# A two-block transformer forward pass on one Trainium2 core: context products ahead of x's, four fixed experts with a ring of 16, and two groups of loads issued inside the attention loop

## What is computed

```python
# first block, for each of 2 layers:
#   x += 0.5 * ffn(rmsnorm(x));  x += attention mix of three branches;  x += 0.5 * ffn(rmsnorm(x))
# x = rmsnorm(x) * final_g
# second block:
hx = _modulate(_rmsnorm(x, norm1_g), sh1, sc1)        # from c @ w_ada
hc = _modulate(_rmsnorm(ctx, norm1_g), csh1, csc1)    # 256 context tokens, from c_ctx @ w_ada
qa, ka, va, qr, kr, vr, gr = split(hx @ w_in)         # x: all seven parts
ka_c, va_c, kr_c, vr_c = parts of split(hc @ w_in)    # context: the parts that x attends to
x_new = x + gt1 * (concat([attention(qa, [ka_c, ka], [va_c, va]), retention(...)]) @ w_out)
y = _hier_moe(_modulate(_rmsnorm(x_new, norm2_g), sh2, sc2), ...)  # top-1 group, top-2 of its 8 experts
out = _rmsnorm(x_new + gt2 * y, final_norm_g)
```

## Time and profile before

| | |
|---|---|
| median of 3 runs | 2082.81 us (2081.47 to 2091.58) |
| the profiled execution's own time | 2081.88 us |
| its span | 2080.1 us |
| PE busy | 1984.5 us (95%) |
| DVE busy | 1132.3 us (54%) |
| ACT busy | 655.0 us (31%) |
| loaded and stored by DMA | 475.56 MB, mean 229 GB/s |

### The profile page before, as it was taken

The page is one execution under the profiler, slowest core; times in us unless marked ns, Lnnn a source line. Parts: engine busy times, 40 slices in busy tenths (PEclk is TensorE's granted clock), DMA queues, the critical chain, the costliest instruction groups (busy, mean ns, idle before and its releaser), DMA issues.

```text
span 2080.1 us, 33242 instructions
## 1 busy us (share of the span) xinstructions
PE 1984.5 (95%) x13991; PEld 1629.1 (78%) x13991; DVE 1132.3 (54%) x1939; ACT 655.0 (31%) x980; POOL 0.2 (0%) x4
## 2 busy tenths in 40 slices
PE   7999999998999999999999999979997998989997
PEld 7999998887999999999888999968665444434443
DVE  6665669845655665666984556554475222222222
ACT  4433436614333533343661433320332000000001
POOL 0000000000000000000000000000000000000000
PEclk9999999999999999999999999999899999999999
DMA  7798553448776677655244877612305999999995
GB/s 223 246 356 244 170 172 95 132 132 233 223 220 194 205 220 215 196 170 173 92 132 135 260 222 214 166 41 81 142 23 203 421 422 420 422 420 422 421 421 246
DMA packets 273950, 475.56 MB, mean 229 GB/s; under 512 B 28182, under 2 KB 234064, under 8 KB 249224
## 3 DMA queue, kind: packets, MB, share of 16 engines
q1 hardware_dynamic: 267148, 471.75, 65.8%
q10 hardware_dynamic: 6652, 1.65, 0.6%
HBM read 472.22 MB, written 7.95 MB: 231 GB/s over the span
## 4 chain that ended last, share of the span: by engine, by line
PE 78%; DMA 16%; DVE 3%; ACT 1%; ACTq 1%; issue 0%; SPq 0%; DVEq 0%
PE ps L692 77%; DMA ring_zone<-in_moe_w_up_dram 16%; PE ps L992 1%; ACTq L395 1%; PE ps L1128 0%; DVE hl L1706 0%; DVE xT L1713 0%; DVE WL L1695 0%; DMA PT<-in_norm_g_dram 0%; SPq L618 0%; ACT WH L1370 0%; DVE xT L1758 0%; ACT gT L1501 0%; DVE xT L1889 0%; DVE h2l L2266 0%
## 5 line engine op out<-in xcount | busy, mean ns | idle before, releaser
L1695 DVE TENSOR_TENSOR WL<-W,WH 128x1024 fp32r<-128x1024 f32 x372 | 452.3, 1223 | 324.7 <-ACT WH L1370 324.3
L692 PE MATMUL ps<-hh,WH 128*128 128x256 f32 x2128 | 604.7, 284 | 18.8 <-DVE WL L1695 13.1
L692 PE MATMUL ps<-hl,WH 128*128 128x256 f32 x2128 | 595.8, 280 | 0.0
L692 PE MATMUL ps<-hh,WL 128*128 128x256 f32 x2128 | 595.4, 280 | 0.0
L1370 ACT ACTIVATE WH<-W 128x1024 fp32r<-128x1024 f32 x372 | 391.0, 1056 | 469.1 <-PE ps L692 429.0
L692 PEld LDWEIGHTS ps<-hh,WH 128*128 128x128 f32 x2128 | 401.8, 189 | 32.5 <-issue 21.1
L692 PEld LDWEIGHTS ps<-hl,WH 128*128 128x128 f32 x2128 | 401.9, 189 | 0.2
L692 PEld LDWEIGHTS ps<-hh,WL 128*128 128x128 f32 x2128 | 401.6, 189 | 0.0
L692 PE MATMUL ps<-ring_over,XT 128*64 128x512 f32 x896 | 228.2, 594 | 31.0 <-DMA ring_zone<-in_moe_w_up_dram 14.3
L692 PEld LDWEIGHTS ps<-ring_over,XT 128*64 128x64 f32 x896 | 77.1, 137 | 176.1 <-issue 176.0
L692 PE MATMUL ps<-hid_h,WH 128*128 128x256 f32 x704 | 200.5, 285 | 0.0
(11 more groups left out here) (330 smaller groups left out, 2194.9 us busy)
## 6 DMA issues: line engine op xcount, KB each, us to landing
ring_over<-in_moe_w_gate_dram SPq DMA_DIRECT2D x64, 1024.0 KB, 20.4
ring_zone<-in_moe_w_down_dram SPq DMA_DIRECT2D x64, 1024.0 KB, 18.8
ring_over<-in_moe_w_up_dram SPq DMA_DIRECT2D x48, 1024.0 KB, 22.5
W<-in_ffn_w_gate_dram SPq DMA_DIRECT2D x88, 512.0 KB, 4.9
W<-in_ffn_w_up_dram SPq DMA_DIRECT2D x88, 512.0 KB, 4.4
W<-in_ffn_w_down_dram SPq DMA_DIRECT2D x88, 512.0 KB, 3.9
W<-in_w_in_dram SPq DMA_DIRECT2D x78, 512.0 KB, 4.4
W<-in_w_gate_dram SPq DMA_DIRECT2D x48, 512.0 KB, 3.7
```

Source lines behind the costliest of these rows:

```text
L692: ins = nc.tensor.matmul(o, lhsT, rhs, start=start, stop=stop, skip_group_check=True, **kw)
L1695: v.tensor_tensor(low, W[:, i % RAW, :], high.bitcast(F32), ALU.subtract).then_inc(low_ready, 1)
```

## The change

Three edits, made together.

1. **Context first.** The context is loaded into `gT`, normed, transposed and modulated inside `ffn(1, 1)`, blocks 5 to 7, and split into `hc_h` and `hc_l`. `w_in2` becomes a split kind, so that all 13 products are `mm3`. They run in the order of `ORDER`, which begins with the context's 3 and 6. The two norms of x are made one: `block_squares` forms the squares of x and of x times its gain, `block_sums` adds both up, and `modulated` makes the high and low part of the modulated x. The normed x itself (`normed_residual`) is made later, after the product at position 5. `decay(0)` moves ahead of the last two products.
2. **Four fixed experts, 16 places.** Blocks 0 to 3 belong to experts 0 to 3. `RING` is 16: one place more in the zone, and `hl`, `mT`, `hT` as places. SP waits for the table only at piece 24. The position of a token's slot no longer needs the running sum over experts (tokens beyond the 64th of an expert get a number far away); the running sum moves into `block_table`, and `move_tokens` gives slots their true numbers after the first quad.
3. **Loads.** Layer 1's `load_na` is issued by SP within the pieces of `w_branch` of layer 0; the first two `ada_unit`s of `ffn(l, 1)` are issued among the pieces of `w_o`.

```diff
-RING, RING_OVER, RING_RAW = 12, 7, RAW // 2
+RING, RING_OVER, RING_ZONE, RING_RAW = 16, 7, 6, RAW // 2
+ORDER = (3, 6, 2, 5, 8, 7, 0, 1, 4, 11, 12, 10, 9)
+CHUNK = {0: 0, 1: 1, 2: 2, 3: 2, 4: 3, 5: 4, 6: 4, 7: 5, 8: 5, 9: 6, 10: 6, 11: 7, 12: 8}
+SIDE = {1: [("ss", 3)], 3: [("ss", 2)], 4: [("rot", 2)], 5: [("rot", 5)], 7: [("ss", 0)], 8: [("ss", 1), ("rot", 0)],
+        9: [("rot", 1)], 10: [("rot", 4)]}
+CONTEXT_AT = 5
+RESIDUAL_AT, DECAY_AT = 5, 10
-SPLIT = ("ffn_gate", "ffn_up", "ffn_down", "w_in", "w_gate")
+SPLIT = ("ffn_gate", "ffn_up", "ffn_down", "w_in", "w_gate", "w_in2")
 # SP
                     if n == RING_OVER:
                         sp.wait_ge(m_ready, 2 * KD + 4)
+                    if n == RING_OVER + RING_ZONE - 1:
+                        sp.wait_ge(lg_ready, 2)
+                    if n == RING - 1:
+                        sp.wait_ge(x_turned, 1)
...
+                    if kind == "w_o" and half == 0 and c % 2 == 0:
+                        load_ada(first_ada(key, 1) + c // 2)
+                    if plan[i] == ("w_branch", 0, 8, 0):
+                        sp.wait_ge(qk_free, NA_H)
+                        load_na(sp, 1)
...
-            first_experts(range(RING_OVER, RING))
+            first_experts(range(RING_OVER, RING_OVER + RING_ZONE - 1))
             first_experts(range(RING_RAW))
+            first_experts(range(RING_OVER + RING_ZONE - 1, RING))
+            fixed_end = plan.index(("moe_gate", FIXED, 0, 0))
+            stream(moe_at + RING, fixed_end)
             sp.wait_ge(table_ready, 1)
 # PE, in ffn
+                    if (l, i, b) == (1, 1, CONTEXT_AT + 1):
+                        turn_context()
 # PE, second block
+            pe.wait_ge(ctx_low, 4)
+            sums = begin()
+            turns.step()
+            for p, g in enumerate(ORDER):
+                c = CHUNK[g]
+                bank = begin()
+                if p == CHUNK_FIRST[c]:
+                    held[c] = [take("w_in2")]
+                product(held[c], bank, g, 0)
+                if p == 0:
+                    block_sums(sums)
+                if p == CHUNK_FIRST[c]:
+                    held[c].append(take("w_in2"))
+                product(held[c], bank, g, 1)
+                idx[g] = turns.step()
+                if p == CHUNK_LAST[c]:
+                    done_pair(2)
 # ACT
+            def block_squares():
+                nc.scalar.activation(rt[:, 2, 1:2], eps[:, :], ACT.Sqrt)
+                for b in range(4):
+                    act.wait_ge(x_tiles, due(x_tiles))
+                    for k in (2 * b, 2 * b + 1):
+                        nc.scalar.activation(nT[:, k, :], xT[:, k, :], ACT.Square, scale=col("final_g", k))
+                    nc.scalar.activation(mT[:, 2 * b:2 * b + 2, :], xT[:, 2 * b:2 * b + 2, :], ACT.Square)\
+                        .then_inc(sq_ready, 1)
...
+            def round_modulated():
+                for k in range(KD):
+                    act.wait_ge(h_plain, due(h_plain))
+                    nc.scalar.activation(hh[:, k, :], nT[:, k, :], ACT.Identity, bias=MOD[:, k, 0:1])\
+                        .then_inc(norm_h, 1)
...
-                if l + 1 < DEPTH:
-                    load_na(act, l + 1)
 # DVE
+            def modulated():
+                take()
+                dve.wait_ge(rms, due(rms))
+                give(v.reciprocal(rstd[:, :], rstd[:, :]))
+                given()
+                for k in range(KD + 1):
+                    if k < KD:
+                        v.scalar_tensor_tensor(out=nT[:, k, :], in0=xT[:, k, :], scalar=G1[:, 0, k:k + 1],
+                                               in1=rstd[:, :], op0=ALU.mult, op1=ALU.mult).then_inc(h_plain, 1)
+                    if k:
+                        dve.wait_ge(norm_h, due(norm_h))
+                        v.scalar_tensor_tensor(out=hl[:, k - 1, :], in0=nT[:, k - 1, :], scalar=MOD[:, k - 1, 0:1],
+                                               in1=hh[:, k - 1, :].bitcast(F32), op0=ALU.add, op1=ALU.subtract)\
+                            .then_inc(h_ready, 1)
```

## The result

The changed kernel takes 2051.52 us (median of 4 runs, 2049.62 to 2052.42), the one before 2085.24 us beside it (4 runs, 2081.47 to 2091.58): ratio 0.984, 95% interval 0.982 to 0.986, 1.6% faster. The forecast was 2033 us with a range of 2018 to 2047. The direction is right; the time lies 4.5 us above the range. The profiled execution takes 2051.78 us with a span of 2050.0, 30.1 us less than before, where the prediction has 49.5.

The account below looks back on a forecast made before the run. PE was taken as the bound up to the experts, the DMA stream of expert weights from there. Terms -9.5 + 5.5 - 28.3 - 6 - 2.6 - 8.6 = -49.5 from 2081.88 gave 2032.4, predicted 2033 us, range 2018 to 2047.

Parts of the forecast that it names:

- loads of tables: Start of `ffn(0, 1)`: issuing the loads from SP ends PE's wait for the split; -9.5 us, bounds -9.5 and 0.
- context into `ffn(1, 1)`: Context's transposes, router row and a 2.3 us wait added in `ffn(1, 1)`; +5.5 us, bounds +3.3 and +9.
- feed-forward's end to last product: Last feed-forward matmul to end of 13 split products: 125.8 us become 97.5; -28.3 us, bounds -33 and -18.
- attention's start: Last product to first retention product: decay matrices already made, later steps perhaps at higher clock; -6 us, bounds -3 and -9.
- routing: From expert counts to slots, five of DVE's 16 operations remain; -2.6 us, bounds -3 and -1.5.
- expert stream: Expert weights: restart 3.9 us after the first expert matmul, 172 pieces instead of 176; -8.6 us, bounds -13 and -4.
- rival B: Experts: stream not started earlier, through late places or loads; only routing's -2.6 stays of the end; 2041 us, chance 0.08.
- A: Projections bound by DVE, splits behind side work; 2043 us with the -18 bound, chance 0.17.
- C: Layer 1's table loads on SP delay the branch weights, PE waits up to 8 us; 2041 us, chance 0.07.
- D: Faster: no late split (-5.1) and no wait in block 6 (-2.3); 2025 us, chance 0.12.
- the wait in block 6: In `ffn(1, 1)`, bank turns tie PE to DVE while the context is transposed; PE waits 2.3 us.
- E: Slower: more than 32 expert blocks, so eight more run, 48 pieces, 120 us; about 2152 us, chance 0.02.

Follow-up runs that it names:

- the square first: Changed kernel with ACT squaring piece 3 before its eight roundings of the modulated x, instead of after; 2034.53 us, ratio to the kernel before 0.976.
- -32: Square moved first, `eps` and `eps_sq` in one tile, `neglam` and `subg` in one: later tiles 32 bytes lower than in the kernel before; 2058.31 us.
- -96: Square moved first, `eps`/`eps_sq` in one tile, `neglam`, `subg`, `rstd_of`, `rtok` in one: later tiles 96 bytes lower than in the kernel before; 2024.81 us.
- its shifted twin: Changed kernel with one more unused 4-byte tile behind `eps_sq`, later tiles 64 bytes higher than in the kernel before; 2072.50 us.

## Why the prediction was wrong

By its steps, forecast and measured in the profiled executions:

| step | forecast | measured |
|---|---|---|
| loads of tables | -9.5 | -9.45 |
| context into `ffn(1, 1)` | +5.5 | +4.8 |
| feed-forward's end to last product | -28.3 | -17.9 |
| attention's start | -6 | -5.1, and +0.8 up to the routing |
| routing | -2.6 | -1.9 |
| expert stream | -8.6 | -6.9 |
| equal work in the first block | 0 | +4.4 |
| start of the program | 0 | +1.1 |

- **Feed-forward's end to last product** is the step that failed, by 10.4 us, and beyond its own bound of -18. Its order of events came true: product 2 starts 22.1 us behind the last hidden matmul, as forecast, PE waits 3.6 us there (forecast 4.3), and late splits and a late `Z` cost 3.5 (forecast 5.1). What the step did not have is the clock, a term that it put at nothing. It costed every matmul at full rate although it put an idle stretch of its own ahead of ten products. The half clock took 9.0 us in products 2 and 5 (23.15 against 14.17) and 1.5 in one at 1441 (7.26 against 5.73 for 48 matmuls). The earlier trace rows show 0.88 and 0.79 behind PE's idle stretches: the rows were there, and no term was made of them. With the wait gone the stage gives -37.8 to the first retention product, 3.7 of them the wait itself; the other -34.1 are the -33.9 that the prediction has for the same stretch. So the order of events and the waits were right, and the clock was the missing term. That the remainder meets the forecast to 0.2 us is partly luck: the waits came out 2.3 us shorter than forecast (3.6 and 3.5 against 4.3 and 5.1), and the work between them longer by about as much.
- **Attention's start**: the 7.8 us are 2.7 (forecast 2.2). The 1.5 us that a higher clock should have given came out as a loss of 0.8, since the clock fell at 1469 for 6.8 us; with the square first the stretch gives 2.4 (98.3 us against 100.7).
- **Equal work** had no term and cost 4.4 us, set by 32 bytes in the list of tiles. No row of the kernel before prices it.
- **Expert stream**: 1.7 us short. The restart came 4.5 us behind the first expert matmul, not 3.9, and the 172 pieces took 437.8 us, 3.7 more than 428.4 + 5.7 instead of the 3 forecast. A fault that doesn't show in the sum is the price of the restart: the term counts 1.7 us for it (3.9 instead of 5.6) and rival B puts the loss of the early start at 8.6, while the runs show 1.0 us for a restart 5.0 us later, within the scatter. The places are worth 8.7.
- **Tables, context, routing** were right within 0.7 us. In the routing, DVE's chain gave its 2.5 us (from the count to the gather 5.8 us, 8.3 before), but the gather that follows took 5.9 instead of 5.4, a larger part of it at half clock. PE waits nowhere between 440 and 510. SP was held 16 us by the 16 transfers (11 forecast), within its lead.
- **Rivals.** A (DVE the bound) is out: moving two items took most of the waits away. B and C did not occur: the restart came before the table, and no branch weight was late. D neither: late splits and `Z` cost 3.5 us and the wait in block 6 0.9 (2.3 forecast). E neither: there are 64 gate transfers again.

## What to carry to other kernels

When a forecast puts an idle stretch of some us on TensorE, price the matmuls behind it at the lower clock as a second case; the wait may be the smaller part, and reordering one 0.4 us instruction, or filling the stretch with needless matmuls, can win more than the wait. Take out such waits first, and then look for late work on the vector engine. When equal work gets slower everywhere by a per cent after an edit, compare the addresses of the tiles before looking for anything else.

## What was not expected of the hardware

- The pace of the split matmuls changes when tiles move in SBUF by 32 bytes: 192.9 to 198.6 us for the same stage at the same clock, up to 34 us from the first root to the last hidden matmul (1341.4 us at -32 against 1307.3 at -96). No rule for the best place came out of seven places; the tiles of the zone decide, and that is all that is shown.
- One idle stretch of 3.56 us went with 20.5 us at half clock with PE busy for 20.0 of them, in three kernels alike (the changed one, its shifted twin, and the one with the tables on ACT). Longer waits had shorter falls: in the kernel before, the waits of 7.32 and 5.67 us went with 6.8 us each. What sets the length is open.

```profile
494.60:501.40 6.80, 4.23 (x20) 4.23 (x21) 4.63 (x4) 5.57 (x6) 0.00 (x0) 0.50 1.00 211
1375.20:1382.00 6.80, 4.04 (x10) 3.26 (x11) 6.73 (x19) 0.00 (x0) 0.00 (x0) 0.50 0.00 0
```

- Short waits are a matter of chance as far as the traces tell: each of the 18 has a wait of some 1.5 us for `hl` at three places of the first block (near 214, 685 and 885 us), and behind 15 of these 54 waits a fall of 3.4 us begins within 2.2 us. A wait of 2.2 us later on was followed by a fall in some kernels and by none in others with the same order.
